# Layer 2's lifting tiles in three split passes, raw head tiles in its first projection, another order of dots and of the wide up tiles

## The reference

```python
def hybrid_layer(x, c, pos, ...):
    mod = (silu(c) @ w_ada + b_ada)[:, None, :]
    shift_a, scale_a, gate_a, shift_f, scale_f, gate_f = split(mod, 6)
    h = rms_norm_2(x, attn_norm) * (1.0 + scale_a) + shift_a
    (nq, nkc, nvc, nks, nvs, nkw, nvw, ngate, cq, ckv, kr, bgate) = split(h @ w_in)   # 1024 -> 5336
    q_a = rope(rms_norm_2(heads(nq, 8), nsa_q_norm), pos)
    kc = rms_norm_2(compress(rope(heads(nkc, 2), pos), cmp_k_pe, cmp_k_w1, cmp_k_w2), nsa_kc_norm)
    vc = compress(heads(nvc, 2), cmp_v_pe, cmp_v_w1, cmp_v_w2)    # silu(flat @ w1) @ w2
    ...                                                           # sparse attention -> o_a
    q_b = (rms_norm_2(cq, mla_cq_norm) @ w_uq)                    # 384 -> 8 heads x 192
    kv_b = (rms_norm_2(ckv, mla_ckv_norm) @ w_ukv)                # 256 -> 8 heads x (128 + 128)
    q_b, k_b = rms_norm_2(q_b, mla_q_norm), rms_norm_2(k_b, mla_k_norm)
    ...                                                           # rope, attention -> o_b
    x = x + gate_a * ((sigmoid(bgate_a) * o_a + sigmoid(bgate_b) * o_b) @ w_o)
    ...                                                           # a second norm and a convolved FFN
```

## Time and profile before

| | |
|---|---|
| Time, median of three runs | 1669.01 us (1669.0 to 1669.76) |
| The profiled execution: its own time, its span | 1670.53 us, 1668.7 us |
| Mean granted PE clock | 0.999 |
| Busy PE, PE's weight loads | 1628.9 us (98%), 1433.9 us (86%) |
| Busy DVE, ACT, POOL | 1246.0 us (75%), 822.4 us (49%), 165.2 us (10%) |
| Chain of waits that ended last, by engine | PE 84%, DVE 7%, ACT 6%, DMA 2% |
| DMA | 316.97 MB, 190 GB/s in the mean |

### The profile page before, as it was taken

One profiled execution on the slowest core, in us unless ns is written; L12 is line 12 of the kernel. 1 busy time (PEld: TensorE's weight loads), 2 busy tenths in 40 slices (PEclk: granted clock), 3 DMA queues, 4 the chain that ended last, 5 costly groups with the idle time before them and its releaser, 6 DMA issues.

```text
span 1668.7 us, 32597 instructions
## 1 busy us (share of the span) xinstructions
PE 1628.9 (98%) x11564; PEld 1433.9 (86%) x11564; DVE 1246.0 (75%) x2630; ACT 822.4 (49%) x1492; POOL 165.2 (10%) x135
## 2 busy tenths in 40 slices
PE   6999999999999999999999999999999999999998
PEld 4887988899988887888888888888899777999998
DVE  6885538759989888788888888888446565588887
ACT  3544111364469844555555555555544246544443
POOL 0020000017700000000000000000037214100000
PEclk9999999999999999999999999999999999999999
DMA  8842135865742287777777777777454651245553
GB/s 346 292 144 90 41 117 202 322 194 176 220 134 69 95 259 264 231 233 239 233 239 234 238 236 235 239 234 232 149 175 137 218 183 39 90 143 185 180 185 126
DMA packets 102624, 316.97 MB, mean 190 GB/s; under 512 B 11392, under 2 KB 21376, under 8 KB 102144
## 3 DMA queue, kind: packets, MB, share of 16 engines
q1 hardware_dynamic: 101664, 311.27, 57.0%
q10 hardware_dynamic: 864, 4.39, 0.7%
HBM read 309.71 MB, written 5.90 MB: 189 GB/s over the span
## 4 chain that ended last, share of the span: by engine, by line
PE 84%; DVE 7%; ACT 6%; DMA 2%; issue 1%; POOL 0%; SPq 0%; DVEq 0%; ACTq 0%
PE bank L499 9%; PE bank L500 9%; PE bank L501 9%; PE bank L514 9%; PE bank L2060 7%; PE bank L2062 6%; PE bank L2064 6%; PE bank L515 4%; PE bank L1293 3%; ACT arena L2023 2%; PE bank L474 2%; PE bank L1579 2%; ACT arena L2014 2%; PE bank L740 2%; PE bank L1696 1%; PE bank L1860 1%
## 5 line engine op out<-in xcount | busy, mean ns | idle before, releaser
L493 DVE TENSOR_TENSOR wlo<-wring,whi 128x1024 fp32r<-128x1024 f32 x340 | 414.1, 1223 | 74.7 <-ACT whi L488 66.1
L488 ACT CAST whi<-wring 128x1024 fp32r<-128x1024 f32 x386 | 403.7, 1046 | 122.4 <-PE bank L2064 48.9
L499 PE MATMUL bank<-xboth,whi 128*128 128x256 f32 x1112 | 319.5, 287 | 3.8 <-DVE wlo L493 2.7
L500 PE MATMUL bank<-xboth,whi 128*128 128x256 f32 x1112 | 314.5, 283 | 0.0
L501 PE MATMUL bank<-xboth,wlo 128*128 128x256 f32 x1112 | 314.5, 283 | 0.0
L514 PE MATMUL bank<-xboth,whi 128*128 128x512 f32 x616 | 220.8, 397 | 0.0
L499 PEld LDWEIGHTS bank<-xboth,whi 128*128 128x128 f32 x1112 | 213.1, 192 | 8.7 <-DVE wlo L493 3.9
L500 PEld LDWEIGHTS bank<-xboth,whi 128*128 128x128 f32 x1112 | 213.3, 192 | 0.7 <-issue 0.5
L501 PEld LDWEIGHTS bank<-xboth,wlo 128*128 128x128 f32 x1112 | 213.2, 192 | 0.0
L493 POOL TENSOR_TENSOR wlo<-wring,whi 128x1024 fp32r<-128x1024 f32 x46 | 117.6, 2562 | 833.5 <-ACT whi L488 833.3
L515 PE MATMUL bank<-xboth,wlo 128*128 128x256 f32 x616 | 172.7, 280 | 0.0
(11 more groups left out here) (401 smaller groups left out, 2857.7 us busy)
## 6 DMA issues: line engine op xcount, KB each, us to landing
wring<-in_w SPq DMA_DIRECT2D x463, 512.0 KB, 3.9
arena<-in_ada SPq DMA_DIRECT2D x48, 512.0 KB, 7.6
xn<-in_ada SPq DMA_DIRECT2D x96, 256.0 KB, 3.3
h_spill<-arena SPq DMA_DIRECT2D x37, 128.0 KB, 2.0
arena<-h_spill SPq DMA_DIRECT2D x37, 128.0 KB, 4.3
wring<-in_w SPq DMA_DIRECT2D x6, 384.0 KB, 4.5
wring<-in_w SPq DMA_DIRECT2D x8, 256.0 KB, 3.2
arena<-in_const ACTq DMA_DIRECT2D x1, 1215.0 KB, 5.5
```

The costliest lines, as they stand in the source:

```text
L488: act.copy(whi[:, n % HSLOTS, :], wring[:, n % SLOTS, :]).then_inc(hi_ready, 1)
L493: eng.tensor_tensor(wlo[:, n % SLOTS, :], wring[:, n % SLOTS, :], whi[:, n % HSLOTS, :].bitcast(F32), ALU.subtract).then_inc(lo_ready, 1)
L499: pe.matmul(out, h, xh, start=start, stop=False, **kw)
L500: pe.matmul(out, h, xl, start=False, stop=False, **kw)
```

## The change

Four things change.

1. *Lifting tiles.* The 14 tiles uk, uq and uv are split tiles, in three passes. `act_lift_hi(j)` makes the upper half of lifting tile j on ACT; it waits for the tile's landing. The first three are made beside the last w_in2 tiles, that of tile j+3 right behind the copy-out of tile j. `lift_lo` makes the lower parts on DVE, at the places of `dve_mla` that the diff shows. The ranks are cut too, by `act_ranks_upper` and `dve_ranks_rest`.
2. *w_in2.* Its five plain tiles go last. The first ten split ones are raw; two of them (in banks 5 and 6) are multiplied block by block while the residual is added, between the sums of the norm, and the warm-up matmuls go. DVE scales the raw tiles and makes the norm's activation and their lower parts between (`w_in2_start`); POOL makes the lower parts of tiles 13 to 31. The places of sums, gives and turns move by four tiles.
3. *Wide up tiles.* `wide8` waits for the upper half, issues seven matmuls of 512 columns, waits for the lower part, issues the eight of 256 and the last of 512.
4. *Head.* The last pair of modulation weights is loaded in swapped order on semaphores of its own, its dots are swapped too, and the four pairs of lower halves come behind all dots.

```diff
@@ constants: which tiles are split, how many of w_in2 are raw
-SPLIT = ["w_in", "wq", "peer", "w_in2", "w_o", "ffn"]
+SPLIT = ["w_in", "wq", "peer", "w_in2", "lift", "w_o", "ffn"]
+LIFT = [tile for tile in MIX if tile[0] in COUNT]
 EARLY = 40
 EARLY_SPLIT = 27
 EARLY_PLAIN = 14
-SKIP = {"w_in": 4, "w_in2": 5, "peer": EARLY}
+SKIP = {"w_in": 4, "peer": EARLY}
+RAW2 = KT + 2
+HEADS2, SPLIT2 = 22, 32
...
-RAWNORMS = (1, )
+RAWNORMS = (1, 2, )
...
+        split_tiles = [MIX_AT[LIFT[k]] if name == "lift" else FIRST[name] + k
+                       for name in SPLIT for k in range(dict(w_in2=SPLIT2, lift=len(LIFT)).get(name) or COUNT[name])
...
@@ wide up tiles
-        def wide8(pe, out, n):
+        def wide8(pe, out, n, split):
+            def upper(k):
+                return pe.matmul(out, whi[:, n % HSLOTS, k * 128:k * 128 + 128], xboth[:, k, :, :],
+                                 start=(k == 0), stop=(k == KT - 1))
+            pe.wait_ge(hi_ready, split)
+            for k in range(KT - 1):
+                upper(k)
+            pe.wait_ge(lo_ready, split)
             for k in range(KT):
-                h, l = whi[:, n % HSLOTS, k * 128:k * 128 + 128], wlo[:, n % SLOTS, k * 128:k * 128 + 128]
-                if k < KT - 1:
-                    pe.matmul(out, h, xboth[:, k, :, :], start=(k == 0), stop=False)
-                    pe.matmul(out[:, 0:S], l, xhi[:, k, :], start=False, stop=False)
-                else:
-                    pe.matmul(out[:, 0:S], l, xhi[:, k, :], start=False, stop=False)
-                    mm = pe.matmul(out, h, xboth[:, k, :, :], start=False, stop=True)
-            return mm
+                pe.matmul(out[:, 0:S], wlo[:, n % SLOTS, k * 128:k * 128 + 128], xhi[:, k, :], start=False, stop=False)
+            return upper(KT - 1)
...
@@ head of the kernel (SP, then DVE)
-            for k in range(2, KT):
+            for k in range(2, KT - 1):
                 pair(k)
+            sp.dma_start(hring[:, 2 * KT - 1, :], a["ada"][2 * KT - 1]).then_inc(side_loaded, 16)
+            sp.dma_start(hring[:, 2 * KT - 2, :], a["ada"][KT - 1]).then_inc(pair_landed[KT - 1], 16)
...
-                dve.wait_ge(pair_landed[k], 32)
-                for vec in range(2):
+                if k < KT - 1:
+                    dve.wait_ge(pair_landed[k], 32)
+                for vec in (0, 1) if k < KT - 1 else (1, 0):
+                    if k == KT - 1:
+                        dve.wait_ge((pair_landed[k], side_loaded)[vec], 16)
...
-            x_rest_pair(dve, 0, 0)
             dots(6)
             known(6, 7)
-            x_rest_pair(dve, 0, 2)
             dots(7)
             known(7, 8)
-            x_rest_pair(dve, 0, 4)
-            x_rest_pair(dve, 0, 6)
+            for k in range(0, KT, 2):
+                x_rest_pair(dve, 0, k)
...
@@ head of w_in2 (pe_peer, dve_peer, then pe_w_in2)
-            for m in range(KT):
-                norm_sum(pe, 2, m, nsq[2])
-            pe_warm(pe, 7, 13)
+            n = FIRST["w_in2"]
+            pe.wait_ge(lo_ready, nth_split[n + 1])
+            for k in range(KT):
+                pe.wait_ge(x_lo, XLO[2] + k + 1)
+                for i in range(2):
+                    mm = raw_three(pe, bank[5 + i], n + i, k)
+                    if k == KT - 1:
+                        mm.then_inc(tile_done, 1)
+                norm_sum(pe, 2, k, nsq[2])
...
+                if m == 1:
+                    raw_shift_rest(dve, 2, 0, 6)
+                if m:
+                    raw_rest(dve, 2, m - 1)
+            raw_rest(dve, 2, KT - 1)
...
-            for k in range(5):
-                n, r = first + k, ring0 + k
-                pe.wait_ge(landed[n % SLOTS], count_at(n))
-                pe.wait_ge(ring_free, r - BANKS + 1)
-                matmul8_tokens(pe, bank[r % BANKS], n % SLOTS, 2 if k == 0 else None).then_inc(tile_done, 1)
-            pe.wait_ge(x_lo, XLO[3])
-            ring_tiles_split(pe, "w_in2", 5, SUMS_AT)
+            for t in range(2, RAW2):
+                pe.wait_ge(lo_ready, nth_split[first + t])
+                if t >= 2 + BANKS:
+                    pe.wait_ge(ring_free, ring0 + t - BANKS + 1)
+                raw8(pe, bank[(ring0 + t) % BANKS], first + t).then_inc(tile_done, 1)
+            pe.wait_ge(x_lo, XLO[3] - 1)
+            ring_tiles_split(pe, "w_in2", RAW2, SUMS_AT)
             pe_nsa_sums(pe)
             ring_tiles_split(pe, "w_in2", SUMS_AT, GIVE_AT)
             pe_nsa_give(pe)
             pe_nsa_turn(pe)
             ring_tiles_split(pe, "w_in2", ROT_AT, RANK_AT)
             pe_rank_sums(pe)
-            ring_tiles_split(pe, "w_in2", RANK_AT, COUNT["w_in2"])
-        SUMS_AT, GIVE_AT, ROT_AT, RANK_AT = 18, 20, 23, 29
+            ring_tiles_split(pe, "w_in2", RANK_AT, SPLIT2)
+            pe.wait_ge(xn_ready, 3 * KT)
+            for k in range(SPLIT2, COUNT["w_in2"]):
+                n, r = first + k, ring0 + k
+                pe.wait_ge(landed[n % SLOTS], count_at(n))
+                pe.wait_ge(ring_free, r - BANKS + 1)
+                matmul8_tokens(pe, bank[r % BANKS], n % SLOTS).then_inc(tile_done, 1)
...
+        SUMS_AT, GIVE_AT, ROT_AT, RANK_AT = 14, 16, 19, 25
...
@@ end of act_w_in2
+                if k == SPLIT2 + 1:
+                    act_ranks_upper(act)
+                if k > SPLIT2 + 1:
+                    act_lift_hi(act, k - SPLIT2 - 2)
...
@@ lifting tiles: the two helpers, and where they are called
+        def act_lift_hi(act, j):
+            if j < len(LIFT):
+                n, w = MIX_AT[LIFT[j]], WIDTH[LIFT[j][0]]
+                act.wait_ge(landed[slot_of(n)], count_at(n))
+                act.wait_ge(tile_done, n - 5)
+                act.copy(whi[:, n % HSLOTS, 0:w], wring[:, slot_of(n), 0:w]).then_inc(hi_ready, 1)
+        def lift_lo(dve, *js):
+            for j in js:
+                n, w = MIX_AT[LIFT[j]], WIDTH[LIFT[j][0]]
+                dve.wait_ge(hi_ready, nth_split[n])
+                dve.tensor_tensor(wlo[:, slot_of(n), 0:w], wring[:, slot_of(n), 0:w], whi[:, n % HSLOTS, 0:w].bitcast(F32),
+                                  ALU.subtract).then_inc(lo_ready, 1)
+        def act_ranks_upper(act):
+            act.wait_ge(c_n, 1)
+            act.wait_ge(tile_done, FIRST["w_in2"] + SPLIT2)
+            act.copy(xhi[:, 0:5, :], F2[:, 16:21, :]).then_inc(x_hi, 1)
+        def dve_ranks_rest(dve):
+            dve.wait_ge(x_hi, XHI[3])
+            dve.tensor_tensor(xlo[:, 0:5, :], F2[:, 16:21, :], xhi[:, 0:5, :].bitcast(F32), ALU.subtract).then_inc(x_lo, 1)
+            dve.wait_ge(lo_ready, nth_split[FIRST["w_in2"] + SPLIT2 - 1])
...
+            dve_ranks_rest(dve)
+            lift_lo(dve, 0, 1, 2)
...
             v.did(dve.tensor_tensor(sq14[:, 8, :], F2[:, 21, :], F2[:, 21, :], ALU.mult))
+            lift_lo(dve, 3, 4, 5)
             dve.wait_ge(ring_free, RING0["uk"] + 4)
             dve.tensor_tensor(sq14[:, 0:8, :], kb[:, :, :], kb[:, :, :], ALU.mult).then_inc(head_sq, 1)
+            lift_lo(dve, 6)
             dve.wait_ge(head_rt, 5)
             dve.reciprocal(r2["rs"][:, 0:S], r2["rs"][:, 0:S]).then_inc(head_inv, 1)
             dve.wait_ge(ring_free, RING0["uq"] + 3)
             v.did(dve.tensor_tensor(sq14[:, 0:6, :], qb[:, 0:6, :], qb[:, 0:6, :], ALU.mult))
+            lift_lo(dve, 7, 8)
             for g in range(4):
+                if g == 2:
+                    lift_lo(dve, 9)
                 dve.wait_ge(head_given, 10 + g + 1)
                 v.did(dve.scalar_tensor_tensor(kb[:, 2 * g:2 * g + 2, :], kb[:, 2 * g:2 * g + 2, :], col("mla_k_nope"),
                                                two(GIVEN[1][g]), ALU.mult, ALU.mult))
                 ins.then_inc(l_k, 1)
             dve.wait_ge(ring_free, RING0["uq"] + 6)
             dve.tensor_tensor(sq14[:, 6:12, :], qb[:, 6:12, :], qb[:, 6:12, :], ALU.mult).then_inc(head_sq, 1)
+            lift_lo(dve, 10, 11)
             dve_compressed_sums(dve, v)
+            lift_lo(dve, 12, 13)
...
+            def uk(n, bk):
                 for o in range(2):
                     for k in range(2):
-                        mm = pe.matmul(bk[:, o * S:(o + 1) * S], blocks(slot, 2 * o + k), F2[:, 19 + k, :],
-                                       start=(k == 0), stop=(k == 1))
+                        mm = three(pe, bk[:, o * S:(o + 1) * S], n, 2 * o + k, xhi[:, 3 + k, :], xlo[:, 3 + k, :],
+                                   k == 0, k == 1)
                 return mm
...
-                pe.wait_ge(landed[slot_of(n)], count_at(n))
+                pe.wait_ge(lo_ready, nth_split[n])
                 pe.wait_ge(ring_free, r - BANKS + 1)
-                dict(uk=uk, uq=uq, uv=uv)[name](slot_of(n), bank[r % BANKS]).then_inc(tile_done, 1)
+                dict(uk=uk, uq=uq, uv=uv)[name](n, bank[r % BANKS]).then_inc(tile_done, 1)
...
+                act_lift_hi(act, t + 3)
...
+                act_lift_hi(act, 4 + t + 3)
...
+                act_lift_hi(act, 10 + t + 3)
...
@@ w_in2 on DVE
```

(27 more changed lines are left out.)

104 lines of the change are left out of this document (67 added, 37 removed).

## The result

The changed kernel takes 1677.69 us (median of five runs, 1674.74 to 1678.6) where the kernel before took 1669.58 beside it: +8.1 us, a ratio of 1.0042 with a 95% interval of 1.0028 to 1.0055. Slower, at the 1678 that was forecast. The profiled execution has a span of 1676.1 us, 7.4 more than the 1668.7 of before.

The account below looks back on a forecast made before the run. PE, which never rests, was taken to bound the kernel. Lifting +12, w_in2's head -2.8, wide tiles -1, head -1.1 and clock +1.5 sum to +8.6: 1678 us on the median, range 1667 to 1687.

Parts of the forecast that it names:

- Lifting, PE's own work: Lifting tiles uk, uq, uv: three split passes save PE 4.9 us, if it never waits.
- Lifting, what has to be ready: Lifting stretch: waits for landings, upper copies and lower parts; steps sum to +13.1 us, taken as +12.
- uk0 to the end of uq1: Start of the lifting stretch: uk3, uq0 and uq1 late by 0.9, 0.7 and 0.7 us; +0.4 us.
- end of uq1 to uq3: Lifting: uq3's lower part follows uq4's landing, root, reciprocal and square; +6.2 us, PE idle for 6.6.
- uv0 to the compressed keys: Lifting: ACT takes uv3's landing and upper copy before the Silu; +3.3 us.
- The 1 us that I took off for less crowded transfers: Lifting: stalled PE leaves DMA less crowded, landings 3 to 3.5 us instead of 4.0, twice; +13.1 becomes +12.
- The head of w_in2: Layer 2's first projection: starting on raw tiles removes the wait for the norm; -2.8 us, bounds -5.0 and 0.
- two waits that I set at 0.8 and 1.4 us: w_in2: PE waits 0.8 us for tile 5's lower part and 1.4 us for the last rest of xn.
- Wide up tiles: 88 up tiles: only the new order of widths counts; -1 us in all, bounds -4 and +6.
- The head: Kernel's head: two lower-half subtractions moved behind the last dot; -1.1 us, bounds -1.4 and 0.
- The clock: Idling before uq3 drops PE to 1.2 GHz for 2 to 3.4 us on the critical chain; +1.5 us.
- the clock falls at every stall: Rival, lifting: three falls at 1.7 us on a chain of +13.1, +13.3 in all, 1682; chance 0.12.

Follow-up runs that it names:

- both orders: Changed kernel with lower parts earlier in DVE's order and two upper copies (uq4, uv3) later in ACT's; 1663.4 us, ratio 0.9966 to the kernel before.
- DVE's order: Changed kernel with only the lower parts of uq3, uq5, uv0, uv1 and uv2 placed earlier on DVE; 1669.3 us, ratio 0.9999 to the kernel before.
- ACT's order: Changed kernel with only uq4's upper copy moved behind the first root and uv3's behind the compressed keys' Silu; 1672.31 us, ratio 1.0012 to the kernel before.
- sums first: Kernel of both orders with second sums, root and reciprocal and uv0's lower part moved earlier; 1661.84 us, ratio 0.9950 to the kernel before.
- PE kept busy: Changed kernel with 26 unused 128-column matmuls in front of uq3; 1674.2 us, ratio 1.0031 to the kernel before.

## Why the prediction was right, and where not

**Lifting, PE's own work.** Right: 4.9 us forecast; in the run with both orders, whose stretch has no fall of the clock, PE's busy time fell by 4.4. In the changed kernel itself the 1.2 GHz hides it (50.12 for 50.50).

**Lifting, what has to be ready.** Its steps, forecast and trace:

| step | before | after | change, forecast | change, traces |
|---|---|---|---|---|
| uk0 to the end of uq1 | 16.5 | 16.1 | +0.4 | -0.4 |
| end of uq1 to uq3 | 5.2 | 11.1 | +6.2 | +6.0 |
| uq3 to uq4 (the clock) | 4.5 | 6.6 | +1.5 | +2.1 |
| uq4 to uv0 | 6.7 | 9.7 | +3.3 | +3.0 |
| uv0 to the compressed keys | 4.8 | 8.2 | +3.3 | +3.4 |
| on to the second give | 5.2 | 5.0 | -0.1 | -0.2 |

The idle time before uq3 was 6.35 us for the 6.6 of the forecast. The first step was off by 0.8: uk3, uq0 and uq1 were 0.5, 0.5 and 0.4 late, not 0.9, 0.7 and 0.7. The 1 us that I took off for less crowded transfers was not to be had at uq4's landing (4.05), where PE's stall had not yet begun; uv3's landing, behind stalls, took 2.96. The fifth row is right by luck: uv0's passes took 2.7 us at 1.2 GHz for the 1.4 of the forecast, and the short landing made up for it. The waits before uq3 and uq5 are confirmed by DVE's order, that before the compressed keys by ACT's order, that before uv0 by sums first, each of which took its wait away; those at the start of the stretch stayed, in part at least, in every run.

**The head of w_in2.** -3.4 us for -2.8, in its bounds. First raw tile and first tile on the finished norm (order of time, all engines, then PE):

```profile
1170.28 0.48 DVE L656 SCALAR_TENSOR_TENSOR raw<-hT,gsc,raw 128x256 fp32r<-128x256 f32 x1
...
1170.91 0.36 PE L505 MATMUL bank<-raw,whi 128*128 128x258 f32 x1 [0.61 <-DVE raw L656]
```

```profile
1204.73 0.39 PE L505 MATMUL bank<-xboth,whi 128*128 128x256 f32 x1 [0.44 <-DVE xboth L701]
```

Raw tiles begin 2.6 us behind the first of PEER's last transposes (1168.3), where the first tile began 9.0 behind it in the kernel before (1182.5, behind 1173.5). Of the two waits that I set at 0.8 and 1.4 us, 0.46 and 0.44 came. This stage is steady: it is 131.0 or 131.1 us in all nine traces with the new w_in2.

**Wide up tiles.** The step "eight at 0.23 and eight at 0.12 are 2.80: -1 us in all" failed in size: 2.772 instead of 2.812, so -3.5, near the bound of -4. I had rounded all distances to 0.01 us (0.227 to 0.23, 2.812 to 2.81), and 88 tiles made 2.5 us of it.

**The head.** Right: -1.2 us at the first split tile of w_in for -1.1. The -2.2 of the stage table is to the first sums, whose start varies by 1.4 us between traces of the same code, and must not be read as double the forecast.

**The clock.** This is the term that was mis-sized: 1.5 us forecast. On the chain uq3, its neighbour and the give took 2.6 us more at 1.2 GHz (2.1 in the table, as three passes save 0.4 there), uv0 1.1 more, and what follows the stretch is 2.1 us longer, with a fall at 1366.7: 5.8 in all. That the last 2 us are the clock's, the other traces show: from the scores to the end it is 311.0 or 311.1 us in the four traces with a fall right behind them (changed kernel, the same with PE kept busy, ACT's order, both orders) and 309.0 to 309.4 in the nine without. The forecast had 2 to 3.4 us at 1.2 GHz, from no row; from uq3's start on it was 5.9. Nor do show an unused PE: it is busy for 2.94 of those 4 us, behind an idle time of 2.46 that ends at 23.06. The rival "the clock falls at every stall" (three at 1.7) came nearer to the price, but not to the places: there were falls at uq3 and uv0, none at the 2.52 us before the compressed keys, and one behind the stretch, which nobody had named. The Trainium skill, "TensorE: Matmul & The Clock Gate", HAM oscillation — how this bites in real kernels, has idle gaps over a certain length throw the array back to half clock; the fall in the 6.35 us gap agrees with it, and it does not tell the gap of 2.50 us, which had a fall, from that of 2.52.

So the time came out at 1678 by errors that work against each other: 3.7 us more gained in head, wide tiles and w_in2 (-8.6 for -4.9; of that 2.5 in the wide tiles, the rest within the scatter of single traces but for 0.6 in w_in2), and 2.5 more lost in and behind the lifting. Within the latter the waits without the clock cost 13.9 - 3.7 = 10.2 us, under the 12 that I took (13.1 as summed), and the clock 5.8 instead of 1.5. The mechanism stands by its waits and their places; that the sum hit 1678 is in part luck.
